# A compression phase and an attention program begin in another order, and a step issues value products before projection ticks

## The reference, cut to what matters

```python
# compress(): 32-row windows of keys and values -> 63 compressed tokens
h = ch[:, :-1] @ w1[:half] + ch[:, 1:] @ w1[half:] + pos_term
return jax.nn.gelu(h) @ w2
...
# project(): one wide projection; its first columns feed the recurrence, its last ones the merge gates
z = rmsnorm(x, p['norm_mix']) @ p['w_in']
...
# nsa_attend(): per query block of 128, 8 heads, three branches
pc = masked_softmax(lc, ...)   # 63 compressed tokens
ps = masked_softmax(ls, ...)   # selected blocks (all blocks here: 16 of 16)
pw = masked_softmax(lw, ...)   # a window of 512
o = g[..., 0:1] * oc + g[..., 1:2] * osel + g[..., 2:3] * ow
...
# lru_branch(): conv over 4 taps, two gates by block-diagonal products, a scan
a = jnp.exp(log_a); b = jnp.sqrt(-jnp.expm1(2.0 * log_a)) * (i * xc)
return h * jax.nn.gelu(gate), ...
```

## Time and profile before

| | |
|---|---|
| three runs | 2702.94, 2691.2, 2700.96 us; median 2700.96 |
| profiled execution | 2694.12 us, span 2692.5 us |
| mean granted TensorE clock | 0.926 |
| TensorE busy | 2413.5 us (90% of the span) |
| VectorE, ScalarE, GpSimd busy | 1071.3, 724.3, 656.0 us |

### The profile page before, as it was taken

How to read it: one execution, slowest core, us unless ns; L and a number is a source line. 1 busy time by engine, 2 the same in 40 slices (tenths; PEclk the granted TensorE clock), 3 DMA queues, 4 the chain that set the end, 5 groups by cost and what they waited for, 6 DMA issues and landing times. The chain is left out here.

```text
span 2692.5 us, 37830 instructions
## 1 busy us (share of the span) xinstructions
PE 2413.5 (90%) x14415; PEld 2233.0 (83%) x14415; DVE 1071.3 (40%) x1945; ACT 724.3 (27%) x1319; POOL 656.0 (24%) x399
## 2 busy tenths in 40 slices
PE   7996776989989899899856587999999999999999
PEld 7995446878889788889833577999999999999999
DVE  5464012535345474555433003163333333333333
ACT  5222011233243543644432004232311111111111
POOL 2212001111111010110025001223543444334443
PEclk9997788999999899999778567999999999999999
DMA  5225324214224031120045726332211111111112
GB/s 176 87 79 180 111 59 142 79 54 125 70 69 121 26 109 44 57 62 28 9 108 161 190 68 228 102 126 87 69 43 47 47 47 47 39 47 47 47 46 79
DMA packets 136152, 226.26 MB, mean 84 GB/s; under 512 B 29419, under 2 KB 95099, under 8 KB 135421
## 3 DMA queue, kind: packets, MB, share of 16 engines
q1 hardware_dynamic: 122492, 194.57, 23.4%
q0 software_dynamic: 6560, 25.22, 3.0%
q10 hardware_dynamic: 6976, 4.79, 0.7%
HBM read 176.80 MB, written 55.08 MB: 86 GB/s over the span
## 5 line engine op out<-in xcount | busy, mean ns | idle before, releaser
L1090 PE MATMUL att_facc<-h_hi,att_w_hi 128*128 128x344 f32 x960 | 338.7, 353 | 69.9 <-DVE att_zf L1267 56.8
L2135 PE MATMUL tl_acc<-tl_x_hi,tl_w_hi 128*128 128x344 f32 x1632 | 349.2, 323 | 20.7 <-DVE tl_x_lo L2198 14.0
L2135 PE MATMUL tl_acc<-tl_x_lo,tl_w_hi 128*128 128x344 f32 x1632 | 348.3, 322 | 0.0
L2135 PE MATMUL tl_acc<-tl_x_hi,tl_w_lo 128*128 128x344 f32 x1632 | 346.6, 321 | 0.0
L1090 PE MATMUL att_facc<-h_hi,att_w_lo 128*128 128x344 f32 x960 | 316.0, 329 | 0.0
L1090 PE MATMUL att_facc<-h_lo,att_w_hi 128*128 128x344 f32 x960 | 315.9, 329 | 0.0
L2135 PEld LDWEIGHTS tl_acc<-tl_x_hi,tl_w_hi 128*128 128x128 f32 x1632 | 276.3, 190 | 21.8 <-issue 15.9
L2135 PEld LDWEIGHTS tl_acc<-tl_x_lo,tl_w_hi 128*128 128x128 f32 x1632 | 278.0, 190 | 0.0
L2135 PEld LDWEIGHTS tl_acc<-tl_x_hi,tl_w_lo 128*128 128x128 f32 x1632 | 273.6, 189 | 0.0
L1090 PEld LDWEIGHTS att_facc<-h_hi,att_w_hi 128*128 128x128 f32 x960 | 188.9, 197 | 84.7 <-DVE att_zf L1267 54.5
L2100 POOL TENSOR_TENSOR tl_w_lo<-tl_raw,tl_w_hi 128x1024 fp32r<-128x1024 f32 x64 | 153.9, 2404 | 425.2 <-ACT tl_w_hi L2041 425.2
(11 more groups left out here) (356 smaller groups left out, 4021.1 us busy)
## 6 DMA issues: line engine op xcount, KB each, us to landing
tl_raw<-in_w_ff SPq DMA_DIRECT2D x66, 512.0 KB, 3.6
z<-att_zf SPq DMA_DIRECT2D x120, 172.0 KB, 3.4
att_raw<-in_w_in SPq DMA_DIRECT2D x40, 512.0 KB, 4.2
tl_tmp<-z SPq DMA_DIRECT2D x24, 516.0 KB, 4.3
tl_raw<-in_w_up SPq DMA_DIRECT2D x16, 512.0 KB, 4.0
fr_raw<-in_w_in SPq DMA_DIRECT2D x14, 512.0 KB, 4.8
zn<-fr_x SPq DMA_DIRECT2D x10, 516.0 KB, 2.9
fr_x<-in_xT SPq DMA_DIRECT2D x8, 644.0 KB, 10.3
```

The lines of the kernel that those rows point to most:

```text
L1090: mm = pe.matmul(facc[:, 0:CW], w[:, u % 2, k, :], h[:, k, c * CW:(c + 1) * CW], start=(x == 0), stop=(x == 23))
L2135: mm = pe.matmul(a[:, c, 0:CW], wt[:, s, k, :], x[:, x0, c * CW:(c + 1) * CW], start=first and n == 0, stop=last and n == 2)
```

## The change

In compress, the four `cp` transfers are issued ahead of SP's 24 pages, and `hidden(n)` is split: `prompt(n)` (the products over the prompt) runs before `samples(n)` (those over the pages), and for n = 0 and 1 both prompt parts run before the wait for the pages.

In the joined program, SP issues the cmp keys first of the keys, `w_load(2)` earlier, and `par` and `st` after `w_load(3)`. VectorE starts with `evict(0)`. The decay rates are cut in two: the first three instructions go to iteration J = 1, the rest to J = 4, and ScalarE's exp for them to J = 2. In each step TensorE issues `values(J-1)`, `transposes(J)` and the turns ahead of the ticks, and VectorE issues `accumulate(J-2)`, `maxima(J)`, `coefficient(J-1)` and then the eviction.

```diff
@@ -604,13 +604,12 @@
                 sp.dma_start(w1[:, kv], d["w_c1"][kv]).then_inc(w_in, 16)
                 sp.dma_start(w2[:, kv], d["w_c2"][kv]).then_inc(w_in, 16)
             sp.dma_start(nm[:], d["nm_kc"]).then_inc(w_in, 16)
-            pages(sp, 0)
-
             sp.wait_ge(zr_done, 2)
             for g in range(2):
                 for s in range(2):
                     sp.dma_start(cp[s * HD:(s + 1) * HD, :, g].rearrange("p k a c -> p k (a c)"),
                                  zr[g * HD:(g + 1) * HD, :, s]).then_inc(cp_in, 16)
+            pages(sp, 0)
             sp.wait_ge(kc_done, 1)
             sp.dma_start(d["kcT"], kc[:]).then_inc(c_out, 16)
             sp.wait_ge(o_ev, 6)
@@ -677,11 +676,9 @@
                     mm = pe.matmul(ps_p[:, 0, kv:kv + 1], w1[:, kv, i, :], per["vec"][:, v0 + i:v0 + i + 1],
                                    start=(i == 0), stop=(i == 15))
             mm.then_inc(pos_mm, 1)
-            for part in range(3):
-                pe.wait_ge(pg_in[part], 16 * (CUTS[part + 1] - CUTS[part]))
             pe.wait_ge(cp_in, 64)
 
-            def hidden(n):
+            def samples(n):
                 kv, g = COMBOS[n]
                 s = n % 2
                 if n >= 2:
@@ -689,13 +686,19 @@
                 for half, o in ((0, ps_lo[s]), (1, ps_hi[s])):
                     for a in range(8):
                         c0 = ((kv * 2 + g) * 8 + a) * 8
-                        pe.matmul(o[:].rearrange("p b c -> p (b c)").rearrange("p (i c) -> p i c", c=8),
-                                  w1[:, kv, half * 8 + a, :], pool_x[:, :, c0:c0 + 8], start=(a == 0), stop=(a == 7))
+                        mm = pe.matmul(o[:].rearrange("p b c -> p (b c)").rearrange("p (i c) -> p i c", c=8),
+                                       w1[:, kv, half * 8 + a, :], pool_x[:, :, c0:c0 + 8], start=(a == 0), stop=(a == 7))
+                mm.then_inc(mm_done, 1)
+
+            def prompt(n):
+                kv, g = COMBOS[n]
+                s = n % 2
+                if n >= 2:
+                    pe.wait_ge(sum_done, 2 * (n - 1))
                 for half in range(2):
                     for a in range(8):
-                        mm = pe.matmul(ps_pr[s][:, half, :], w1[:, kv, half * 8 + a, :], cp[:, kv, g, a, :],
-                                       start=(a == 0), stop=(a == 7))
-                mm.then_inc(mm_done, 1)
+                        pe.matmul(ps_pr[s][:, half, :], w1[:, kv, half * 8 + a, :], cp[:, kv, g, a, :],
+                                  start=(a == 0), stop=(a == 7))
 
             def output(n):
                 kv, g = COMBOS[n]
@@ -716,17 +719,23 @@
                     mm = pe.matmul(ps_p[0:NCK, 0, :], hd[:, s, NS], w2[:, 1, :], start=True, stop=True)
                 mm.then_inc(o_mm, 1)
 
-            hidden(0)
-            hidden(1)
+            prompt(0)
+            prompt(1)
+            for part in range(3):
+                pe.wait_ge(pg_in[part], 16 * (CUTS[part + 1] - CUTS[part]))
+            samples(0)
+            samples(1)
             output(0)
             output(1)
-            hidden(2)
+            prompt(2)
+            samples(2)
 
             pe.wait_ge(sq_done, 1)
             pe.wait_ge(o_ev, 2)
             pe.matmul(ps_o[:], nm[:, 0:P], sq[:, 0:NS * NCK], start=True, stop=True)
             pe.matmul(ps_p[:, 0, :], nm[:, 0:P], sq[:, NS * NCK:], start=True, stop=True).then_inc(ms_mm, 1)
-            hidden(3)
+            prompt(3)
+            samples(3)
             output(2)
             output(3)
 
@@ -928,22 +937,24 @@
 
             w_load(0)
             w_load(1)
-            sp.dma_start(par[:], d["par"]).then_inc(par_in, 16)
-            sp.dma_start(st[:], d["st"]).then_inc(par_in, 16)
             q_load(0, 0)
-            for x, src in enumerate((d["zn"][0][:, 0:NP_], d["zn"][1][:, 0:NP_], d["kcT"][:, NS * NCK:])):
+            keys = (d["zn"][0][:, 0:NP_], d["zn"][1][:, 0:NP_], d["kcT"][:, NS * NCK:])
+            for x in (2, 0, 1):
+                src = keys[x]
                 for half in range(2):
                     sp.dma_start(k_raw[x][half * HD:(half + 1) * HD], src.rearrange("(g p) n -> p g n", g=G)).then_inc(k_in, 16)
             sp.dma_start(near[:].rearrange("p g r n -> p (g r) n"),
                          bass.AP(d["dist"].tensor, RMAX - P, [[8 * RLEN - 1, P], [RLEN, 8], [1, 2 * P]])).then_inc(c_in, 16)
             sp.dma_start(strip, bass.AP(d["dist"].tensor, 16 * 40 - 505, [[8 * RLEN - 1, P], [RLEN, 8], [1, 384]])).then_inc(c_in, 16)
+            w_load(2)
             sp.dma_start(v_sel[:], d["vtok"][0].rearrange("t p n -> p t n")).then_inc(c_in, 16)
             sp.dma_start(v_win[:], d["vtok"][1].rearrange("t p n -> p t n")).then_inc(c_in, 16)
             sp.dma_start(v_cmp[:], d["vc"][:, NS, :]).then_inc(c_in, 16)
             sp.dma_start(wmask[:], d["wmask"]).then_inc(c_in, 16)
             sp.dma_start(cmask[:], d["cmask"][:, 56:56 + NCMP]).then_inc(c_in, 16)
-            w_load(2)
             w_load(3)
+            sp.dma_start(par[:], d["par"]).then_inc(par_in, 16)
+            sp.dma_start(st[:], d["st"]).then_inc(par_in, 16)
             for g in range(3 * NU):
                 if chunk_at[g] == -1:
                     z_store(g)
@@ -1100,8 +1111,6 @@
                     scores(J + 1)
                     if J + 1 in gate_at:
                         gate_products(J + 1)
-                for tick in ticks[J]:
-                    filler(tick)
                 if J >= 1:
                     values(J - 1)
                 transposes(J)
@@ -1109,6 +1118,8 @@
                     turn(J // NJ, 0)
                 if J % NJ == 2 and J >= NJ:
                     turn(J // NJ - 1, 1)
+                for tick in ticks[J]:
+                    filler(tick)
             values(NST - 1)
             turn(NB - 1, 1)
             for tick in ticks[NST]:
@@ -1198,8 +1209,6 @@
             act.wait_ge(k_in, 16 * 6)
             for x, keys in enumerate((k_sel, k_win, k_cmp)):
                 act.activation(keys[:], k_raw[x], ACT.Copy).then_inc(k_hi, 1)
-            act.wait_ge(lam_done, 1)
-            act.activation(lam[:, 3], lam[:, 1], ACT.Exp, scale=-1.0).then_inc(lam_ex, 1)
             for u in range(2, NU):
                 if unit_at[u - 2] == -1:
                     w_high(u)
@@ -1222,6 +1231,9 @@
                         q_high(*q_at[J])
                 if J == NST:
                     turned(NB - 1, 1)
+                if J == 2:
+                    act.wait_ge(lam_done, 1)
+                    act.activation(lam[:, 3], lam[:, 1], ACT.Exp, scale=-1.0).then_inc(lam_ex, 1)
                 for n in range(NBLK):
                     recurrence(n, J - SIG[n])
 
@@ -1239,12 +1251,14 @@
                 ins.then_inc(lam_ch, 1)
                 dve.wait_ge(lam_ch, lams[0])
 
-            def decay_rates():
+            def decay_begin():
                 L = par[:, :, L_LAM]
                 dve.wait_ge(par_in, 32)
                 lam_chain(dve.tensor_scalar(lam[:, 0], L, -1.0, None, ALU.mult))
                 lam_chain(dve.tensor_tensor(lam[:, 1], L, lam[:, 0], ALU.max))
                 dve.tensor_scalar(lam[:, 2], lam[:, 0], 0.0, None, ALU.max).then_inc(lam_done, 1)
+
+            def decay_rates():
                 dve.wait_ge(lam_ex, 1)
                 lam_chain(dve.tensor_scalar(lam[:, 4], lam[:, 3], 2.0, None, ALU.add))
                 lam_chain(dve.reciprocal(lam[:, 4], lam[:, 4]))
@@ -1359,11 +1373,11 @@
                     dve.wait_ge(sc_done, 2 * n + t + 1)
                     dve.tensor_tensor(ig[:, t], r[:, t], e_[:, t], ALU.mult).then_inc(y_done, 1)
 
-            decay_rates()
+            evict(0)
             for x, keys in enumerate((k_sel, k_win, k_cmp)):
                 dve.wait_ge(k_hi, x + 1)
                 dve.tensor_tensor(keys[HD:], k_raw[x][HD:], keys[HD:].bitcast(F32), ALU.subtract).then_inc(k_lo, 1)
-            for g in range(3 * NU):
+            for g in range(1, 3 * NU):
                 if chunk_at[g] == -1:
                     evict(g)
             dve.wait_ge(c_in, 16 * 7)
@@ -1371,15 +1385,19 @@
             chain(dve.tensor_copy(cstrip[:].rearrange("p g r n -> p (g r) n")[:, :, 0:24],
                                   strip.rearrange("p h (n x) -> p h n x", x=16)[:, :, :, 0]))
             for J in range(LAST):
+                if 2 <= J < NST + 2:
+                    accumulate(J - 2)
+                if J < NST:
+                    maxima(J)
+                if 1 <= J <= NST:
+                    coefficient(J - 1)
                 for g in range(3 * NU):
                     if chunk_at[g] + 1 == J and J:
                         evict(g)
-                if J < NST:
-                    maxima(J)
-                if 2 <= J < NST + 2:
-                    accumulate(J - 2)
-                if 1 <= J <= NST:
-                    coefficient(J - 1)
+                if J == 1:
+                    decay_begin()
+                if J == 4:
```

(1 more changed line is left out.)

## The result

The changed kernel takes 2754.70 us (median of 4 runs, 2750.41 to 2760.53); the kernel before takes 2696.47 us in the same set (4 runs). The ratio is 1.0214, 95% interval 1.0182 to 1.0245: the change makes the kernel slower by 2.1%. The forecast was 2733 us (2715 to 2755 as stated) with a range of 2692 to 2785, and 0.69 for slower. The profiled execution of the changed kernel took 2750.41 us, 56.3 more than that of before (2694.12).

What follows compares the result with a forecast made beforehand. TensorE, busy for 90% of the span, was taken to bound the kernel. The terms summed to +34.5 us on 2694.12 us profiled or 2700.96 us median, giving 2729 to 2735, stated as 2733 us (2715 to 2755; range with rivals 2692 to 2785).

Steps and rivals of the forecast that it cites:

- Compress: Compress phase: prompt products run before the pages, which TensorE starts 2 us later; gain 5 us, bounds 3 and 6.
- Joined beginning: Start of the joined program: chunk 0's eviction no longer waits behind other VectorE work; gain 16 us, bounds 12 and 18.
- Decay rates at J = 4: Step 4: the decay chain delays maxima and eviction of step 5; cost 4 us, bounds 2 and 6.
- tails -15: Steps 0 to 71: ticks cover most of the recurrence tails' square root, GELU and tanh; gain 15 us, bounds 8 and 24.
- mask products +5.5: Query block 0, steps 5, 8, 11: transposes wait behind an eviction and a convolution step; cost 5.5 us, bounds 2 and 7.
- chain +36: Steps 72 to 172: new VectorE and ScalarE chain between value products leaves TensorE idle; cost 36 us, bounds 20 and 50.
- tails +5: Recurrence tails of blocks 2 and 3: VectorE's and ScalarE's pieces stand in the chain; cost 5 us, bounds -8 and 20.
- rival 3: Late steps: the clock falls with the new gaps, 0.8 in steps 120 to 172; 2765 us, chance 0.14.
- Steps 173 to 191: Steps without ticks: the new chain leaves TensorE idle in cmp and sel steps; cost 20 us, bounds 8 and 34.
- Rival 1: Late steps: the chain stays hidden, so the kernel ends faster, at 2672 us; chance 0.15.
- Rival 2: Whole kernel: gains and losses meet, chain at half cost or beginnings and tails at upper bounds; about 2704 us, chance 0.16.
- Rival 4: Beginnings don't move because the keys land late: 12 us less gain, 2745 us; shares the forecast's chance of 0.55.

Runs made afterwards that it cites:

- steps_only: The kernel before with the new order in TensorE's and VectorE's step and the old beginnings: 2769.98 us, ratio 1.0275 to the kernel before.
- max_first: The changed kernel with VectorE's `maxima(J)` put ahead of `accumulate(J-2)` again: 2684.68 us, ratio 0.9952 to the kernel before.
- copies_first: The changed kernel with ScalarE's copies put ahead of the next exponential: 2682.09 us, ratio 0.9951 to the kernel before.
- dose_after: The changed kernel with one more VectorE maximum over the score tile in each step from 72 on: 2830.49 us, ratio 1.0505 to the kernel before.
- begin_only: The changed kernel with the new beginnings kept and the old order inside a step: 2674.19 us, ratio 0.9911 to the kernel before.
- decay_late: `begin_only` with `decay_rates()` at J = 14 instead of 4: 2670.45 us, ratio 0.9911 to the kernel before.
- whigh_later: The changed kernel with ScalarE's high part of the weights one step later, and so GpSimd's low part: 2740.22 us, ratio 1.0181 to the kernel before.
- best: The changed kernel with maxima before accumulate, copies before exponential, and the edits of `whigh_later` and `decay_late`: 2637.37 us, ratio 0.9787 to the kernel before.

## Why the prediction was right, and which terms were off

The direction, and the mechanism that decides it, were right: a chain from one value product to the next over VectorE's sum and maximum and ScalarE's exponential and copy, from step 72 on. `steps_only` shows it alone, `max_first` and `copies_first` cut it at each of its two joints, and `dose_after` loads it. The size was low: the sum was 34.5 us; between the two profiled executions it is 56.3, and the measured 2754.70 us lies at the upper end of the forecast. The two large misses (the tails in steps 0 to 71 and the clock) both point to slower, so the range was not met by errors that cancel. One term, the tails, had the wrong sign.

- **Compress: predicted -5 (bounds -3 and -6), measured about -6.2.** TensorE's last product there ends at 376.6 instead of 383.6, and the phase began 0.8 us earlier in this execution. The pages' issue ended at 299.2 and TensorE began on them 1.7 us later; I had taken 3. SyncE's 24 issues kept their 35 us.
- **Joined beginning: predicted -16, measured -15.8** (step 0 22.8 us earlier, less the 7.0 of compress). The idle time of TensorE was 5.25 us where 5.1 was said.
- **Decay rates at J = 4: predicted +4 (2 to 6), measured +5.3** as the difference of `begin_only` to before in steps 0 to 23. The two traces divide it. TensorE waits 4.1 us for the eviction instead of 1.9, once for 2.5 us, the late eviction that I had named; and the same 742 instructions keep it busy for 3.1 us longer at a lower clock, which `decay_late` has too (126.8 us):

```profile
449.30:588.90 139.60, 123.73 (x742) 112.00 (x742) 53.55 (x182) 34.56 (x101) 22.35 (x12) 1.00 0.28 83
```

```profile
427.80:572.80 145.00, 126.88 (x742) 115.15 (x742) 58.63 (x213) 35.96 (x103) 22.33 (x12) 0.97 0.27 80
```

So 2.2 us, near the lower bound, are the chain's own, and the rest is the clock, which my term did not have; why it is lower there no run shows.
- **Steps 0 to 71, tails -15 and mask products +5.5: predicted -9.5 together, measured +1.1** (`steps_only` against before; with the new beginnings the two parts together cost 7.8, 3.8 more than singly). This term came out with the wrong sign. The idea held: with the high part a step later (`whigh_later`, against `begin_only`) the same steps show -9.2. What failed is the step "in the new one they start before the ticks of step J": where a unit ends, ScalarE's recurrence piece stands behind `w_high`, which waits for the last of these ticks (24.2 us in 15 waits, none before), so the square root and the GELU start after the ticks, not under them. And `w_high` starts GpSimd's subtraction, now in the same microsecond as VectorE's convolution. I had not asked which instruction in ScalarE's list waits for the moved ticks, nor what GpSimd would run beside VectorE. The wait for `transposes(23)` came out at 4.95 us, as said.
- **Steps 72 to 172, chain +36 and tails +5: predicted +41, measured +52.9.** Of this +34.7 is idle time, so the idleness was priced rightly, a little high. The rest, 18.3 us, is nearly the same work done more slowly, most of it by the lower granted clock, which my sum left at nothing and put into rival 3. By query block, the chain alone as predicted against all that was measured: block 3 +5 and +7.5, block 4 +4 and +6.4, block 5 +10 and +14.3, block 6 and the start of 7 +16.5 and +24.6. In this last one TensorE waits 17.5 us, 20 times, and has a clock of 0.96 where it was 1.00. The value products waited in about half of the steps, not in two of three.
- **Steps 173 to 191: predicted +20 (8 to 34), measured about +22.7.** Idle time grows from 10.4 to 28.8 us, and the rest is busy time at 0.65 instead of 0.73 of the clock.

**The rivals.** Rival 1 (the chain hidden, 2672) fell: the value products wait 62 us in steps 72 to 173. Rival 2 needed the chain at half its price; idle time alone was 34.7. Rival 3 was right in kind and about half in size: slower work took 18 us, most of it by the clock, in query blocks 3, 5 and 6, and none of them fell to 0.8. Rival 4 fell: the keys' copies began at 399.0, which with the 7.0 us of compress is 406.0, against the 405.5 that I took.

The terms measured sum to -6.2 - 15.8 + 7.8 + 52.9 + 22.7 = +61.4, which is the 60.6 of the joined program's end and the 0.8 of the earlier start. My sum was 27 us low against it: 13 in steps 0 to 71, 12 in steps 72 to 173 (mostly the clock) and 3 in the last ones, less 1 in compress. Between the profiled executions 22 are left, since the rest of the program was 4 us shorter and the phase began 0.8 us earlier in that of the changed kernel; the median is 22 us above the forecast as well.

## What to carry to other kernels

When work is moved on one engine, write down for every other in-order engine what now stands between its input and the next thing that the first one waits for; a loop that closes over two engines costs in each turn, and cutting it at either joint gives nearly all back (70 of 75 us here), at both joints more. A reorder that looks bad as a whole can hold a good part: the same TensorE order with VectorE's maximum and ScalarE's copy ahead of their neighbours is, with the new beginnings, 2.1% faster than the kernel before. And look in every other engine's list for the instruction that waits for the moved work: here one copy of weights on ScalarE did, and what stood behind it, the recurrence's pieces, waited with it. Then list what GpSimd starts on that copy, and what VectorE does in that same microsecond.

## What the hardware showed that was not expected

A VectorE instruction of 8 columns takes 0.22 us alone and up to 2.37 us while GpSimd subtracts two 128x1024 tiles (2.41 us alone, 2.86 where it starts inside VectorE's 1024-wide instruction). In the rows above GpSimd waits out the rest of VectorE's instruction, and the next instruction of VectorE waits until GpSimd is done. The Trainium skill (SBUF — State Buffer, "Who interferes with whom") says that a VectorE instruction with two SBUF inputs and a GpSimd instruction that reads SBUF share a pair of ports, that whichever is first holds it for its whole instruction and that the other is fully blocked. The ends at 646.02 and 646.05 agree with that, as far as they go: the profile's spans of GpSimd are rough.

The same code up to compress starts compress at dates up to 5 us apart in different executions (`cp` issued at 259.70 us in after and at 265.01 in `best`), so a step's date is to be compared only with that taken off.
